# An expert block's 64 places dealt over eight groups of eight, in place of filled from the lowest

## The chip, the cores and the metric

The kernel runs on one core of one Trainium2 chip. The metric is the device time of one execution, in microseconds (us). Before the change three runs gave 1841.0, 1848.68 and 1850.56 us, median 1848.68 us.

## What is computed

Two layers of a transformer-like block in float32: 512 latent tokens and 256 context tokens of width 1024 go through convolutions, attention and a mixture of experts. Only the mixture matters here. Each token picks one of 4 groups and in it 2 of 8 experts; the tokens are sorted by expert, each expert's rows are padded to whole blocks, and each block goes through that expert's three matrices:

```python
eid = (grp[:, None] * N_PER_GROUP + top_i).reshape(-1)
order = jnp.argsort(eid)
...
buf = jnp.zeros((n_blocks * MOE_BLOCK, shp[-1]), t.dtype).at[dest].set(t[tok_sorted])
...
hdn = jax.nn.silu(xb @ e_gate[e]) * (xb @ e_up[e])
return hdn @ e_down[e]
...
y = ybuf[dest] * gate.reshape(-1)[order][:, None].astype(t.dtype)
out = jnp.zeros_like(t).at[tok_sorted].add(y)
```

The first layer has 768 tokens (1536 rows for experts), the second 512 (1024 rows). In which place of its block a row stands has no influence on the result.

## The kernel before

**Blocks.** A block has B = 64 places. An expert gets one block for each 64 rows, at least one. A row of 1024 numbers is cut into two halves of 512 (2 KB each): the half 0 of place r stands in SBUF partition r, the half 1 in partition 64 + r, so a block fills the tile `xg` of 128 partitions by 512 numbers. With the router's choices on the given inputs the blocks hold these numbers of rows, in the order in which they are worked on (an expert with more than 64 rows has several blocks):

```
first layer, 38 blocks: 47 33 41 51 41 23 41 39 61 22 64 2 38 64 40 64 30 64 64 37 36 29 26 24 38 15 32 25 21 54 45 35 64 7 59 55 50 55
second layer, 33 blocks: 21 35 55 19 46 37 12 39 46 33 3 28 64 12 54 33 21 8 28 62 48 16 42 1 43 24 14 17 22 61 41 6 33
```

**Routing** (`route`, lines 1437 to 1515, on VectorE). Every row gets a destination: its block, and its place in the block, `dest_r`, which counts 0, 1, 2 ... in the order of the rows. A one-hot table `hot_r` (line 1488) has a column for each place; it compares `dest_r` with the constant `slot`, whose column c holds c. A matmul of `hot_r` with a second table `hot_q` gives `list_gather` and `list_scatter`: for each of the 128 partitions and each block, the number of the half row that stands there. A place that no row fills gets a number out of bounds.

**Expert loop.** For each block, TensorE (`experts`, from line 916) multiplies by gate, up and down, taking turns with the transposes of the next block's `xg` (line 920). GpSimd gathers the rows of the block after that from HBM (line 1953, the list copied by line 1950) and scatters the results `y_rows` to HBM (line 1961), each with one indirect DMA of 128 partitions. Indices out of bounds move nothing:

```python
po.indirect_dma_start(out=xg, out_offset=None, in_=h2_dram[layer],
                      in_offset=bass.IndirectOffsetOnAxis(ap=idx_gather[:, 0:1], axis=0),
                      bounds_check=2 * tiles * P - 1, oob_is_err=False).then_inc(gathered[layer], 16)
```

**Weights.** SyncE loads each expert's gate, up and down (2 MB each, line 493) into nine slots, three experts' worth; the slots of expert e are loaded again for expert e + 3 as soon as the last block of expert e has been through that matrix (`reload`, line 504). TensorE waits for each piece in `weights_in`. A DMA is split over 16 DMA engines and is done when the last of them is; the indirect DMAs use the same 16 engines through a queue of their own.

Of the kernel before, what the change touches and what calls it, by code (L numbers as in the profile page):

```python
# [13 lines left out]
P = 128  # L14
# [5 lines left out]
XT, CT = S // P, C // P  # L20
NT = XT + CT
TOK = S + C
HD = 64
# [3 lines left out]
NE = NG * NPG  # L27
DE = 512
B = 64
# [8 lines left out]
CONST = {}  # L38
_at = 0
for _name, _width in (("ident", P), ("ones", P), ("before", P), ("mask_prev", P), ("mask_next", P),  # L40
                      ("cos", XT * HD), ("sin", XT * HD), ("slot", B), ("name", NE),
                      ("token", NT), ("half", 1), ("select", 2), ("eps", 1)):
    CONST[_name] = (_at, _width)
    _at += _width
# [110 lines left out]
def hybrid_flow_block(nc, x, ctx_tokens, conditions, consts, smalls, rows, w_mod, w_in, w_out, w_router,  # L155
                      e_gate, e_up, e_down, out):
    stack = ExitStack()
    with stack:
# [60 lines left out]
        hot_r = r2[:, 4608:5376].rearrange("p (a r) -> p a r", a=2 * NT)  # L219
# [63 lines left out]
        def cst(name):  # L283
            a, n = CONST[name]
            return const[:, a:a + n]
# [71 lines left out]
        def tiles_of(layer):  # L357

            return NT if layer == 0 else XT
# [675 lines left out]
        def _(ve):  # L1035
# [401 lines left out]
            def route(layer):  # L1437

                t = tiles_of(layer)
# [45 lines left out]
                nc.vector.tensor_tensor(hot, hot, value.rearrange("p c i -> p (c i)").unsqueeze(2).to_broadcast([P, 2 * t, width]),  # L1485
                                        ALU.mult).then_inc(hot_q_ready, 1)
                for c in range(2):
                    nc.vector.tensor_tensor(hot_r[:, c * t:(c + 1) * t, :], cst("slot").unsqueeze(1).to_broadcast([P, t, B]),
                                            dest_r[:, c * t:(c + 1) * t].unsqueeze(2).to_broadcast([P, t, B]),
                                            ALU.is_equal).then_inc(hot_r_ready, 1)  # L1490
                own(nc.vector.tensor_scalar(blk_table[0:1, 0:NE + 1], begins[0:1, :], 1.0 / B, None, ALU.mult))
# [88 lines left out]
            for layer in range(DEPTH):  # L1580
# [46 lines left out]
                for i in (tiles - 2, tiles - 1):  # L1627
                    choose_first(layer, i)
                    choose_second(layer, i)
                route(layer)  # L1630
                experts(layer)
                if layer == DEPTH - 1:
# [377 lines left out]
def shape_constants():  # L2010

    import numpy as np

    c = np.zeros((P, N_CONST), np.float32)

    def put(name, values):
        a, n = CONST[name]
        c[:, a:a + n] = values

    p = np.arange(P, dtype=np.float32)[:, None]  # L2020
    f = np.arange(P, dtype=np.float32)[None, :]
    put("ident", p == f)
    put("ones", 1.0)
    put("before", p < f)
    put("mask_prev", np.where(f < p, NEG, 0.0))
    put("mask_next", np.where(f > p, NEG, 0.0))
    half = HD // 2
    inv = np.float32(ROPE_THETA) ** (-np.arange(0, half, 2, dtype=np.float32) / np.float32(half))
    token = np.arange(S)
    ar = (token // GRID_W).astype(np.float32)[:, None] * inv  # L2030
    ac = (token % GRID_W).astype(np.float32)[:, None] * inv
    angle = np.concatenate([ar, ar, ac, ac], axis=-1)
    sign = np.tile(np.repeat(np.float32([-1, 1]), half // 2), 2)
    put("cos", np.cos(angle).reshape(XT, P, HD).transpose(1, 0, 2).reshape(P, -1))
    put("sin", (np.sin(angle) * sign).reshape(XT, P, HD).transpose(1, 0, 2).reshape(P, -1))
    put("slot", np.arange(B))
    put("name", np.arange(NE) - 1000)
    put("token", p + P * np.arange(NT) + 1)
    put("half", p // B)
    put("select", (p % 32) == np.arange(2))  # L2040
    put("eps", EPS)
    return c
# [66 lines left out]
```

## Time and profile before

| what | value |
|---|---|
| median of 3 runs | 1848.68 us |
| the profiled execution, its own time | 1849.2 us |
| its span, first to last instruction | 1847.6 us |
| TensorE busy | 1621.6 us (88%) |
| share of the chain that ended last: TensorE / DMA | 63% / 27% |
| expert loop of the first layer | about 520 to 1006 us |
| expert loop of the second layer | about 1357 to 1822 us |

In the profile, the chain follows the program back from its end: at each step to the work that released it. The DMA line shows the mean busy share of the 16 DMA engines in tenths, the line of GB/s below it what they moved. In a window of the DMA view, the packets of each queue are counted with their bytes and with the time they took as a share of 16 engines; q1 carries the weights, q0 the gathers and scatters.

### The profile page before, as it was taken

What the parts mean: (1) busy time and instruction counts of PE and PEld (TensorE: products, weight loads), DVE (VectorE), ACT (ScalarE), POOL (GpSimd) and SP (SyncE); (2) the same over time, 40 slices, a digit from 0 to 9 for tenths busy, and PEclk for the clock granted to TensorE, in tenths of its full rate; (3) what the DMA queues carried; (4) which work ended last, traced back from release to release, by engine and by line L of the source; (5) the groups of instructions that cost most, each with busy time, mean ns of one, the idle gap of its engine ahead of it and who ended that gap; (6) DMA issues with size and microseconds to landing.
All of it is one profiled execution on the core that took longest, in us unless ns stands there. A gap on an engine that the chain in (4) does not pass through costs nothing.

```text
span 1847.6 us, 27090 instructions
## 1 busy us (share of the span) xinstructions
PE 1621.6 (88%) x9896; PEld 942.9 (51%) x9897; DVE 647.8 (35%) x1643; ACT 310.9 (17%) x709; POOL 219.7 (12%) x346
## 2 busy tenths in 40 slices
PE   5999998999779899999796899899879979787784
PEld 3555445744456556665453444575446546344442
DVE  2094645533722222222122776552531111111113
ACT  4111115731200000000000411372300000000000
POOL 0000000000012122222111000000012112111111
PEclk9999999999879999999999899999979999999997
DMA  9358146021569999899998702302479999999995
GB/s 386 168 207 369 67 205 277 5 69 68 203 266 426 427 424 426 339 425 426 427 425 340 301 0 96 132 1 75 181 292 426 425 426 425 426 427 425 427 425 205
DMA packets 55001, 530.67 MB, mean 287 GB/s; under 512 B 12056, under 2 KB 12728, under 8 KB 25504
## 3 DMA queue, kind: packets, MB, share of 16 engines
q1 hardware_dynamic: 37760, 492.26, 63.7%
q0 software_dynamic: 14432, 27.15, 3.9%
q10 hardware_dynamic: 2752, 10.49, 1.5%
q8 instruction: 38, 0.62, 0.1%
q14 instruction: 19, 0.16, 0.0%
HBM read 520.85 MB, written 26.28 MB: 296 GB/s over the span
## 4 chain that ended last, share of the span: by engine, by line
PE 63%; DMA 27%; DVE 7%; ACT 2%; issue 1%; ACTq 0%; SPq 0%; POOLq 0%; DVEq 0%
PE ps L932 24%; DMA ring<-in_e_down_dram 13%; DMA ring<-in_e_up_dram 11%; PE ps L655 10%; PE ps L688 7%; PE ps L878 5%; PE ps L734 3%; PE ps L782 3%; PE ps L605 3%; PE ps L803 2%; DMA r<-y_dram 1%; PE ps L920 1%; PE ps L969 1%; DVE r L1531 1%; PE ps L627 1%
## 5 line engine op out<-in xcount | busy, mean ns | idle before, releaser
L932 PE MATMUL ps<-ring,r 128*64 128x256 f32 (+1 forms) x3888 | 535.7, 431 | 71.9 <-DMA ring<-in_e_up_dram 34.4
L932 PEld LDWEIGHTS ps<-ring,r 128*64 128x64 f32 x3888 | 312.1, 139 | 279.9 <-issue 132.2
L932 PE MATMUL ps<-r 128*64 128x256 f32 (+1 forms) x1768 | 241.0, 425 | 30.9 <-DMA r<-in_e_up_dram 14.8
L1528 DVE TENSOR_TENSOR r<-r,ps 128x128 f32<-128x128 f32 x142 | 34.4, 284 | 541.6 <-PE ps L932 541.6
L932 PEld LDWEIGHTS ps<-r 128*64 128x64 f32 x1768 | 142.5, 138 | 121.3 <-issue 54.5
L655 PE MATMUL ps<-r,ring 128*128 128x512 f32 (+1 forms) x480 | 177.9, 530 | 3.7 <-ACT r L1671 2.1
L688 PE MATMUL ps<-ring,r 128*128 128x512 f32 (+1 forms) x384 | 158.4, 567 | 0.0
L878 PE MATMUL ps<-ring,r 128*128 128x512 f32 x320 | 142.9, 603 | 0.8 <-DVE r L1324 0.8
L655 PEld LDWEIGHTS ps<-r,ring 128*128 128x128 f32 x480 | 91.2, 192 | 91.9 <-issue 81.2
L1548 DVE TENSOR_TENSOR r<-ps,r 128x512 f32<-128x512 f32 x71 | 49.1, 692 | 211.2 <-PE ps L932 211.2
L1838 ACT ACTIVATE r<-ps 128x256 f32<-128x256 f32 x71 | 27.2, 383 | 548.2 <-PE ps L932 548.2
L688 PEld LDWEIGHTS ps<-ring,r 128*128 128x128 f32 x384 | 72.8, 194 | 80.4 <-issue 77.5
L1196 DVE SCALAR_TENSOR_TENSOR r<-r,small 128x512 f32<-128x512 f32 (+1 forms) x180 | 104.6, 660 | 0.0
L1961 POOL DMA_INDIRECT y_dram<-r,idx_scatter x71 | 73.6, 1037 | 222.0 <-DVE r L1548 222.0
L878 PEld LDWEIGHTS ps<-ring,r 128*128 128x128 f32 x320 | 60.6, 193 | 73.9 <-issue 72.5
L1953 POOL DMA_INDIRECT r<-h_dram,idx_gather x73 | 86.1, 1180 | 63.4 <-POOL idx_gather L1950 59.6
L1294 DVE TENSOR_REDUCE stat<-ps 128x1 f32<-128x768 f32 (+3 forms) x80 | 61.3, 766 | 63.4 <-PE ps L771 40.3
L1842 ACT COPY r<-ps 128x128 f32<-128x128 f32 x71 | 18.8, 265 | 352.9 <-PE ps L969 352.9
L1950 POOL COPY idx_gather<-list_gather 128x1 uint32 (+1 forms) x73 | 13.4, 183 | 486.9 <-PE ps L920 486.9
L920 PE MATMUL ps<-const,r 128*128 128x128 f32 x292 | 60.4, 290 | 9.9 <-DMA r<-h_dram,list_gather 9.9
L782 PE MATMUL ps<-const,r 128*128 128x128 f32 x368 | 59.1, 291 | 8.9 <-ACT r L1775 4.7
L1775 ACT ACTIVATE r<-ps,stat 128x768 f32<-128x768 f32 (+3 forms) x80 | 60.5, 756 | 15.5 <-DVE stat L1300 8.2
(217 smaller groups left out, 1305.0 us busy)
## 6 DMA issues: line engine op xcount, KB each, us to landing
ring<-in_e_up_dram SPq DMA_DIRECT2D x44, 2048.0 KB, 35.1
ring<-in_e_down_dram SPq DMA_DIRECT2D x44, 2048.0 KB, 35.4
ring<-in_e_gate_dram SPq DMA_DIRECT2D x43, 2048.0 KB, 32.6
ring<-in_w_mod_dram SPq DMA_DIRECT2D x24, 2048.0 KB, 17.7
r<-in_e_gate_dram SPq DMA_DIRECT2D x20, 2048.0 KB, 35.9
r<-in_e_up_dram SPq DMA_DIRECT2D x20, 2048.0 KB, 38.2
r<-in_e_down_dram SPq DMA_DIRECT2D x20, 2048.0 KB, 38.4
ring<-in_w_in_dram SPq DMA_DIRECT2D x8, 2048.0 KB, 20.2
```

Source lines behind the costliest of these rows:

```text
L605: mm = pe.matmul(ps[32 * g:32 * g + 32, mod_bank(n), :], cond[:, 2 * g + k, :], w[:, 2 * g + k, :], start=(k == 0), stop=(k == 1), tile_po ...
L655: mm = pe.matmul(ps[:, (ct % 2) * 2 + j, 0:tn], w[:, k, col:col + P], h1T[:, t0 // P:(t0 + tn) // P, k, :], start=(k == 0), stop=(k == KD ...
L688: mm = pe.matmul(ps[:, 4 + u % 2, c0:512], h1T[:, i, k, :], chunk_ap(layer, n)[:, k, c0:512], start=(k == 0), stop=(k == KD - 1))
L782: mm = pe.transpose(ps_flat[:, 3072 + n * P:3072 + (n + 1) * P], prob[:, u % 2, n * P:(n + 1) * P], ident)
L878: mm = pe.matmul(ps[:, u % 2, :], catT[:, k, i * P:(i + 1) * P], w[:, k, :], start=(k == 0), stop=(k == 7))
L920: return pe.transpose(ps[:, 4, j * P:(j + 1) * P], xg[:, j * P:(j + 1) * P], ident)
L932: mm = pe.matmul(ps[g * B:(g + 1) * B, bank, 0:width], x, w[:, k, g * width:(g + 1) * width], start=(k == first), stop=(k == last), tile_p ...
L1196: ins = nc.vector.scalar_tensor_tensor(out=dst, in0=src, scalar=wt, in1=dst, op0=ALU.mult, op1=ALU.add)
L1294: own(nc.vector.tensor_reduce(stat[:, u % 4, 3:4], ps_flat[:, at:at + len(tiles) * P], AX.X, ALU.max))
L1775: nc.scalar.activation(prob[:, u % 2, 0:n], ps_flat[:, at:at + n], ACT.Exp, bias=stat[:, u % 4, 0:1], scale=SCALE, accum_out=stat[:, u % 4 ...
L1953: po.indirect_dma_start(out=xg, out_offset=None, in_=h2_dram[layer], in_offset=bass.IndirectOffsetOnAxis(ap=idx_gather[:, 0:1], axis=0), b ...
L1961: po.indirect_dma_start(out=y_dram[layer], in_=y_rows, in_offset=None, out_offset=bass.IndirectOffsetOnAxis(ap=idx_scatter[:, 0:1], axis=0 ...
```

## The change

A second constant, `place`, of the same width as `slot`, holds in column c the number c % 8 * 8 + c // 8. The one-hot table of the places compares with it instead of with `slot`. So the row with count v in its block now stands in place (v % 8) * 8 + v // 8: rows 0 to 7 go to the places 0, 8, 16, ... 56, rows 8 to 15 to the places 1, 9, 17, ... 57, and so on. Of n rows, the group of places 8g to 8g + 7 gets those counted g, g + 8, g + 16, ..., from its lowest place on. Gather list, scatter list, and the block in SBUF are permuted alike.

```diff
-                      ("cos", XT * HD), ("sin", XT * HD), ("slot", B), ("name", NE),
+                      ("cos", XT * HD), ("sin", XT * HD), ("slot", B), ("place", B), ("name", NE),
...
-                    nc.vector.tensor_tensor(hot_r[:, c * t:(c + 1) * t, :], cst("slot").unsqueeze(1).to_broadcast([P, t, B]),
+                    nc.vector.tensor_tensor(hot_r[:, c * t:(c + 1) * t, :], cst("place").unsqueeze(1).to_broadcast([P, t, B]),
                                             dest_r[:, c * t:(c + 1) * t].unsqueeze(2).to_broadcast([P, t, B]),
                                             ALU.is_equal).then_inc(hot_r_ready, 1)
...
     put("slot", np.arange(B))
+    put("place", np.arange(B) % 8 * 8 + np.arange(B) // 8)
```

No engine gets another instruction or another order. The one instruction of another size is the first DMA of SyncE, which brings the constants at the start of the program:

```order
 L459 UNCONDITIONAL_BRANCH
-L461 DMA const<-in_consts_dram 128x1258
+L461 DMA const<-in_consts_dram 128x1322
 L462 DMA small<-in_smalls_dram 128x2x162
 L463 DMA cond<-in_conditions_dram 128x256
```

It carries 64 more columns of 128 partitions, 32 KB.

## Rows read from the trace of the kernel before

**Rows 1.** The page, parts 1 and 2: span, and 40 equal slices of it.

```profile
span 1847.6 us, 27090 instructions
...
DMA  9358146021569999899998702302479999999995
```

**Rows 2.** Windows of the expert loops: length, busy time by engine, clock, DMA share, GB/s.

```profile
core 0: us, PE busy (x) PEld busy (x) DVE busy (x) ACT busy (x) POOL busy (x), PEclk, DMA share, GB/s
520.00:757.00 237.00, 225.00 (x1638) 139.53 (x1640) 55.32 (x135) 12.32 (x38) 52.29 (x77) 0.98 0.95 400
...
1400.00:1800.00 400.00, 336.37 (x2406) 190.42 (x2402) 57.84 (x140) 18.12 (x57) 68.48 (x112) 0.99 1.01 426
```

**Rows 3.** Chain in order of time: start, length, what.

```profile
619.48 39.73 DMA ring<-in_e_down_dram
659.25 10.56 PE ps L932 x80
...
894.77 42.08 DMA ring<-in_e_down_dram
...
964.26 36.76 DMA ring<-in_e_down_dram
1001.11 3.67 PE ps L932 x16
...
1764.99 41.76 DMA ring<-in_e_down_dram
```

**Rows 4.** DMA view, end of the second layer's loop, 1798 to 1820 us, 40 slices.

```profile
DMA  9999897898766756455544342222311100000001
GB/s 387 387 447 447 365 439 313 376 406 373 328 298 268 298 238 268 209 238 238 239 179 209 149 179 119 119 119 89 120 75 60 60 22 8 0 0 0 0 0 30
...
q1 hardware_dynamic: 299, 4.23, 45.0%
q0 software_dynamic: 267, 0.19, 2.7%
```

**Rows 5.** DMA view, end of the first layer's loop, 985 to 1008 us.

```profile
DMA  9899999999999999989997998767643321100000
...
q1 hardware_dynamic: 478, 6.82, 69.6%
q0 software_dynamic: 249, 0.21, 2.6%
```

**Rows 6.** DMA view, 740 to 780 us.

```profile
DMA  9999999999663220220033979999989999899999
```

**Rows 7.** DMA view, 1825.55 to 1825.93 us: start of the last scatter (33 rows).

```profile
DMA packets 33, 0.13 MB, mean 350 GB/s; under 512 B 0, under 2 KB 0, under 8 KB 33
...
q0 software_dynamic: 33, 0.13, 90.3%
```

**Rows 8.** DMA view, 524.40 to 524.85 us: start of a gather of 33 rows.

```profile
DMA packets 20, 0.08 MB, mean 182 GB/s; under 512 B 0, under 2 KB 0, under 8 KB 20
```

**Rows 9.** DMA view, 525.25 to 525.40 us: the same gather's last engine.

```profile
DMA packets 3, 0.00 MB, mean 14 GB/s; under 512 B 2, under 2 KB 2, under 8 KB 3
```

**Rows 10.** DMA view, 520 to 1006 us: q0.

```profile
q0 software_dynamic: 6080, 12.19, 6.5%
```

**Rows 11.** Gathers of line 1953: from issue to landing, all of 560 to 980 us.

```profile
DMA to landing us min/median/max: 3.4/8.6/9.1
```

**Rows 12.** The same, for the gather of 2 rows issued at 646.2 us.

```profile
DMA to landing us min/median/max: 8.1/8.1/8.1
```

**Rows 13.** Timeline, 695 to 706 us: issue of a gather of 64 rows, and the transposes that need it.

```profile
695.61 1.31 POOL L1953 DMA_INDIRECT r<-h_dram,idx_gather  x1 [0.84 <-POOL idx_gather L1950]
...
705.21 0.55 PE L920 MATMUL ps<-const,r 128*128 128x128 f32 x3
```

**Rows 14.** The page, part 6: the DMA of the constants.

```profile
const<-in_consts_dram SPq DMA_DIRECT2D x1, 629.0 KB, 4.0
```

## The prediction

> **What bounds the kernel now.** I read the page first: nothing but permuted data passes through the engines, so the question is where DMA decides. The DMA engines are full, at nines, over most of the two expert loops [rows 1]. The windows say how full: from 1400 to 1800 us the sixteen engines are busy all the time (share 1.01) and move 426 GB/s, while TensorE is busy 336 of 400 us at a clock of 0.99 [rows 2]. In the first loop, up to 757 us, DMA has a little air (0.95) and TensorE almost none (225 of 237 us busy) [rows 2]; about 752 to 760 us the engines run dry, because no slot is free [rows 6]. The chain agrees: its steps through weight loads of some 40 us end at 659 us, at 1001 us and at 1807 us, and TensorE goes on right behind them [rows 3]. So three times the end of a weight load sets the time: once early in the first loop, and at the end of each loop.
>
> A weight load ends when the last of its 16 parts ends, and here the view to look at is the end of each loop, where nothing more is queued. From 1798 us on the DMA share doesn't fall at once; it goes down a staircase, 9 to 0 over 15 us [rows 4]: some engines are done at 1801 us, others at 1816.4 us. Yet all had equal shares of the weights. In that window 4.23 + 0.19 MB move; at 426 GB/s all engines together need 10.4 us, so if the work lay evenly they would end at 1808.4 us. The slowest is **8.0 us** behind the mean. The first loop ends likewise: 6.82 + 0.21 MB need 16.5 us, even end 1001.5 us, real end about 1005.1 us (35 slices of 0.575 us), **3.6 us** behind [rows 5]. What differs between engines is the gathers and scatters, and the change deals exactly these anew.
>
> **Which engine carries which places.** Two windows of 33-row transfers tell. The last scatter begins with 33 packets, all of them data and none empty [rows 7]; so does a gather, 20 packets with none under 512 B [rows 8]. A packet is a pair of neighbouring places. Were eight consecutive places one engine's, the engines of places 40 to 63 (six of the sixteen) would have empty pairs alone and begin with these. They begin with data, all sixteen. The last engine of that gather ends on one half-full packet, one empty and its completion [rows 9]: the pair of places 32, 33, then the empty pair 34, 35, and nothing more. So an engine's places end with 32 to 35 as a run of four, behind data. I take it that each engine has two runs of four, at the same place in each 32: 0 to 3 with 32 to 35, 4 to 7 with 36 to 39, and so on, eight engines for each half row.
>
> The size of the staircase tests this. A full pair took 0.903 × 16 × 0.38 us / 33 = 0.166 us [rows 7], a row's half 0.083 us. In the second loop, over the gathers of blocks 3 to 33 and the scatters of blocks 1 to 31, the engine with places 0 to 3 and 32 to 35 carries 352 rows, the mean engine 244: 108 × 0.083 = 9.0 us, measured 8.0. With eight consecutive places, the first engine would carry 470 rows and be 18.8 us behind. In the first loop, counted from where the engines ran dry, 214 against 161 rows: 4.4 us, measured 3.6. Runs of four it is.
>
> The rows leave the pairing of the runs open. The Trainium skill, page "DMA: Bandwidth & Descriptors", section "The descriptor swizzle", states it for a plain transfer over 128 partitions: partitions 0 to 3 with 32 to 35 on engine 0, the next four with 36 to 39 on engine 1, partitions 64 and up on engines 8 to 15. No run here shows it for indirect transfers beyond the runs of four; it is the pairing I took, and it speaks against this change: with it the sum is the one below, with a pairing shifted by one run the second rival's.
>
> **The change part by part.** *The dealing.* Of n rows each group of eight places now fills from its lowest place. Its first four places lie with one engine, its last four with the next; both runs of an engine are then either first fours or last fours. Up to n = 32, eight of the sixteen engines carry everything and eight nothing. The heaviest carried min(4, n) + min(4, n − 32 if positive); it now carries min(4, n/8 rounded up) + min(4, (n − 4)/8 rounded up). For 36 rows and more both give 8; for 25 to 32 it is 7 or 8 in place of 4; at 16 it is 4 and 4, below that less than before (12 rows: 3 in place of 4). Summed over the list of blocks, the heaviest goes from 250 to 277 rows in the first layer and from 186 to 204 in the second. It is the heaviest engine that decides, not the mean: while it has a queue, its own work sets the end.
>
> Only what lies ahead of a deciding wait counts. Up to 659 us (gathers 3 to 12, scatters 1 to 10): 3 + 7 = 10 more rows. From the dry spell to 1001 us (gathers 22 to 38, scatters 20 to 37): 17 + 17 = 34. Second loop, as above: 15 + 17 = 32. Together 76 × 0.083 = **6.3 us**. The early 0.8 us of it isn't lost again in the dry spell, as TensorE is the bound there and shifts whole.
>
> Bounds: a row at the weights' own rate, 2048 B / (426/16 GB/s), costs 0.077 us; by the whole first loop's gathers and scatters, 0.065 × 16 × 486 us for 12.19 MB [rows 10], 0.085 us. The staircases came to 0.82 and 0.89 of what the count gives, which makes 5.2 us the lower end; all 45 rows both ways at 0.085 us, 7.7 us, is the upper.
>
> *Transfers with nothing beside them.* The second layer's first gather (21 rows) has three data packets on its heaviest engine for two, its last scatter (33 rows) four for two: 3 × 0.166 = 0.5 us, both waited for. *Half-full pairs* become more frequent; a half packet costs its half, nothing. *Constants*: 32 KB more on 629 KB in 4.0 us [rows 14], at most 0.2 us, taken as 0.1 us, ahead of the first tokens. *VectorE's compare*: same size and count, nothing. *Other gathers* in the loops: hidden, see the last rival.
>
> Sum 6.3 + 0.5 + 0.1 = 6.9 us by the count; scaled down a little toward the staircases, **+6.5 us**. Against the profiled execution's own 1849.2 us that is 1855.7 us; the median of the runs is 0.5 us lower, so 1855 us.
>
> **Rivals.** *1. The heaviest engine isn't what decides* (later loads give the lag back, or TensorE has slack I didn't see): no change, about 1849 us. For it: TensorE is the bound over half of the loops. Against: the chain's three long loads [rows 3]. *2. Even load after all:* if runs are paired shifted, so that first and last fours share an engine, every engine gets the mean. Then the lags go: 8.0 us, 3.6 us, and before 659 us some 2.6 us (37 rows over the mean × 0.083 × 0.85): up to 14 us, less a small rest, about 1836 us. Against: nothing in rows 7 to 9 suggests a shift. *3. Slower, by the gather's own latency.* The next block's transposes need a gather 9.6 us after its issue (695.61 to 705.21 us) [rows 13]; the longest gathers land in 9.1 us [rows 11]. Now eight engines, not one or two, carry four data packets, each taking turns with weights. If the latest lands 0.5 us beyond that limit in each of some 40 blocks that TensorE bounds, 20 us are lost: 1869 us; below 9.6 us it costs nothing. Against: a gather of 2 rows lands in 8.1 us [rows 12], all with 64 rows, four packets everywhere, within the 9.1 us, and no block after the change carries more.
>
> **How the numbers follow.** A measurement of this kernel can tell about 0.5%, 9.2 us, from no change. Forecast 0.68, rival 1 0.15, rival 2 0.11, rival 3 0.06. Forecast and rival 1 both lie within 0.5%, but for a rest from the runs' spread (1841.0 to 1850.56 us): faster 0.13, same 0.77, slower 0.10. The forecast's bounds with its small terms, +5 to +8 us, make 1854 to 1857 us; with that spread and rival 1 the range is 1846 to 1862 us, leaving out rivals 2 and 3.
>
> **What would show it.** Right: a last scatter of 33 rows that begins with empty packets and has engines with four data packets; a longer staircase at both ends (lags near 10.7 and 6.4 us); TensorE's waits for weights up by some 6 us; gathers within 9.2 us. Wrong: a staircase that is gone and a time near 1836 us (rival 2); transposes waiting for gathers (rival 3); a longer staircase at an unchanged time (rival 1).

## The result, and the profile after

Nine runs of the changed kernel have a median of 1857.63 us, nine of the kernel before 1848.68 us; the ratio is 1.0054 with a 95% interval of 1.0038 to 1.0070. The change makes the kernel slower by 9 us, 0.5%, and the whole interval lies above 1; forecast were 6.5 us. A second measurement (below) gave 1.0047, 1.0031 to 1.0062.

The page after, span and DMA share; the DMA line answers to that of [rows 1]:

```profile
span 1856.0 us, 27090 instructions
...
DMA  9459146011669999799997702302479999999995
```

The chain says where the 8.4 us of span are. From the kernel before, the four steps that bound the two expert loops (start, length, what), then the chain of the kernel after with the steps that answer to [rows 3]:

```profile
517.00 3.32 DMA r<-h_dram,list_gather
...
1006.43 2.72 DMA y_dram<-r,idx_scatter
...
1353.23 2.87 DMA r<-h_dram,list_gather
...
1823.98 2.46 DMA y_dram<-r,idx_scatter
```

```profile
515.04 3.36 DMA r<-h_dram,list_gather
...
617.53 42.02 DMA ring<-in_e_down_dram
659.60 10.56 PE ps L932 x80
...
962.21 37.12 DMA ring<-in_e_up_dram
999.37 5.25 PE ps L932 x32
1005.90 3.67 PE ps L932 x16
1011.22 2.73 DMA y_dram<-r,idx_scatter
...
1358.28 3.03 DMA r<-h_dram,list_gather
...
1773.16 41.71 DMA ring<-in_e_down_dram
...
1832.09 2.73 DMA y_dram<-r,idx_scatter
```

From the first gather to the last scatter the first loop took 1006.43 − 517.00 = 489.4 us, now 496.2 us (+6.8); the second 470.8, now 473.8 us (+3.1). What lies ahead of the first loop became 2 us shorter, which is chance (below). Within the first loop, 142.25 us passed up to the matmuls behind the early wait (659.25 − 517.00), now 144.56 us (+2.3), and from there to the last down matmuls 341.9, now 346.3 us (+4.4).

The staircase at the end of the second loop (DMA view, 1800 to 1830 us, slices of 0.75 us; it answers to [rows 4]) shows the mechanism at a glance:

```profile
DMA  9998755575445455554555545454542000000000
...
q1 hardware_dynamic: 372, 5.29, 41.3%
q0 software_dynamic: 400, 0.33, 3.2%
```

It is no staircase any more, but one step: from 1803 to 1824 us the share stays at about a half. By the prediction's count for this loop, eight engines carried 368 to 384 rows, the other eight 100 to 128. The 5.62 MB need 13.2 us at 426 GB/s, an even end would be 1813.2 us; the heavy half is **10.8 us** behind it, where 10.7 were forecast. The same at the end of the first loop (985 to 1008 us before [rows 5], 985 to 1012 us here, slices of 0.675 us), 7.14 MB, even end 1001.8 us, real end about 1009.0 us (the last packet of 16 KB starts at 1008.4 us and takes 0.6 us), 7.2 us behind, 6.4 forecast. Read to the end of its last packet, the first loop before ended at 1005.4 us, 3.9 us behind, where the prediction has 3.6:

```profile
DMA  9999999999999997754455564445555451000000
...
q1 hardware_dynamic: 475, 6.73, 58.6%
q0 software_dynamic: 315, 0.41, 4.2%
```

And the last scatter, again 33 rows, begins with empty packets now, 12 of its first 20, where 33 of 33 held data [rows 7] (DMA view, 1833.70 to 1833.80 us):

```profile
DMA packets 20, 0.03 MB, mean 288 GB/s; under 512 B 12, under 2 KB 12, under 8 KB 20
```

### The profile page after: what moved, and what is told of

Read it like the earlier page. It is cut to its first block, busy times and chain, and to the rows that moved or that the text cites. A ratio compares the mean times of both kernels' runs of the same rounds, so it can differ in the third digit from the quotient of the medians.

```text
span 1856.0 us, 27090 instructions
## 1 busy us (share of the span) xinstructions
PE 1623.1 (87%) x9896; PEld 940.1 (51%) x9897; DVE 647.8 (35%) x1643; ACT 311.4 (17%) x709; POOL 219.9 (12%) x346
## 4 chain that ended last, share of the span: by engine, by line
PE 62%; DMA 27%; DVE 7%; ACT 2%; issue 1%; ACTq 0%; SPq 0%; POOLq 0%; DVEq 0%
PE ps L932 24%; DMA ring<-in_e_down_dram 13%; DMA ring<-in_e_up_dram 11%; PE ps L655 9%; PE ps L688 7%; PE ps L878 5%; PE ps L734 3%; PE ps L782 3%; PE ps L605 2%; PE ps L803 2%; DMA r<-y_dram 1%; PE ps L920 1%; PE ps L969 1%; DVE r L1531 1%; PE ps L627 1%
```

## The experiments

All eight were timed in five rounds against the kernel before. The table has the ratios and, from the chain of each profile, the length of the loops (last scatter's issue less first gather's) and of the stretch up to the matmuls behind the early wait. "Rows" is the count of the prediction for the heaviest engine, first loop (both stretches) and second.

| kernel | rows | ratio (95%) | first loop | of it up to the early wait | second loop |
|---|---|---|---|---|---|
| before | 349 + 352 | 1 | 489.4 | 142.3 | 470.8 |
| constant only | 349 + 352 | 1.0004 (0.9989 to 1.0018) | 490.0 | 142.9 | 470.8 |
| the change | 393 + 384 | 1.0054 (1.0038 to 1.0070) | 496.2 | 144.6 | 473.8 |
| the change again | 393 + 384 | 1.0047 (1.0031 to 1.0062) | 495.0 | 144.3 | 474.3 |
| first loop only | 393 + 352 | 1.0027 (1.0015 to 1.0039) | 496.0 | 144.3 | 470.7 |
| second loop only | 349 + 384 | 1.0021 (1.0008 to 1.0033) | 489.4 | 142.1 | 473.9 |
| from the top | 393 + 384 | 1.0046 (1.0030 to 1.0063) | 493.9 | 144.2 | 474.0 |
| one engine after another | 432 + 470 | 1.0089 (1.0068 to 1.0111) | 495.7 | 143.9 | 478.8 |
| even by runs | 281 + 270 | 0.9956 (0.9939 to 0.9973) | 485.7 | 141.0 | 465.1 |
| even there and back | 262 + 250 | 0.9944 (0.9925 to 0.9963) | 486.3 | 141.2 | 465.6 |

**Even by runs.** The rows are dealt to the eight sets of places that the prediction ascribes to one engine each.

```diff
-    put("place", np.arange(B) % 8 * 8 + np.arange(B) // 8)
+    run = np.arange(B) // 4 % 8
+    turn = np.arange(B) % 4 + 4 * (np.arange(B) // 32)
+    put("place", turn * 8 + run)
```

> The change's table replaced by one that deals the rows in turn to eight sets of eight places, a set being two runs of four: 0 to 3 with 32 to 35, 4 to 7 with 36 to 39, and so on. Theory A (the engine with the most rows ends each weight load last; an engine carries two runs of four at the same place in each 32): in the three stretches counted the heaviest engine carries 108 + 173 + 270 = 551 rows in place of 701 before and 777 with the change, so 150 x 0.083 = 12.5 us less than before, 18.8 us less than the change; the staircase at the end of the second loop shrinks to a lag of some 2 us. Theory B (what the change costs is the gathers' own landing, for which TensorE waits): the kernel before has no such wait, so this one is no faster than before; near 1849 us. Theory C (any dealing that isn't consecutive costs): slower than before, like the change.

1838.67 against 1847.25 us: faster than before, so theories B and C fall. The end of its second loop (1785 to 1815 us, slices of 0.75 us):

```profile
DMA  9999999999999989999998856200000000000004
...
q1 hardware_dynamic: 512, 7.34, 57.6%
q0 software_dynamic: 471, 0.43, 4.2%
```

The engines end together, 7.77 MB would do so at 1803.2 us, the last at about 1805.2 us: 2.0 us behind. That bears out that an engine's places are a run of four in the first 32 and one in the last 32 (with eight consecutive places an engine, this dealing would leave 12.6 us by the count). It doesn't say which two runs share an engine: with the pairing shifted by any number of runs, the heaviest engine has 258 to 270 rows in the second loop. "One engine after another" below tells the pairings apart. The gain, 8.6 us by the medians, is less than the 12.5 us of the count.

**Constant only.**

```diff
-    put("place", np.arange(B) % 8 * 8 + np.arange(B) // 8)
+    put("place", np.arange(B))
```

> The extra constant is kept, but holds 0 to 63, so the rows stand as before. Theories A and B: as before within 0.2%, at most 0.2 us for the 32 KB. Theory D (part of the 9 us comes from the longer constants or from what they shift): slower by a few us.

No difference, and loops as before to 0.6 us. Theory D falls: it is the dealing.

**One engine after another.**

```diff
-    put("place", np.arange(B) % 8 * 8 + np.arange(B) // 8)
+    run = np.arange(B) // 4 % 8
+    turn = np.arange(B) % 4 + 4 * (np.arange(B) // 32)
+    put("place", run * 8 + turn)
```

> The opposite dealing: the first eight rows all go to the places 0 to 3 and 32 to 35, the next eight to 4 to 7 and 36 to 39, and so on. Theory A: heaviest engine 154 + 278 + 470 = 902 rows against 701 before: 201 x 0.083 = 16.7 us slower than before, about 1865 us, and a staircase at the end of the second loop of some 19 us of lag. Theory B: the fullest engine has four data packets per gather from eight rows on, as in a full block: no more than the change, 0 to 9 us. Theory C: about the same as the change.

16.4 us slower by the ratio, 16.7 expected, 14.3 us by the medians. Its staircase (1785 to 1830 us, slices of 1.125 us) is the longest of all:

```profile
DMA  9999799797676665565544434222221110000000
...
q1 hardware_dynamic: 608, 8.75, 46.4%
q0 software_dynamic: 560, 0.60, 3.7%
```

9.35 MB, even end 1806.9 us, last weights about 1823.3 us: 16.4 us behind. Put side by side for the second loop: the lags are 2.0, 8.0, 10.8 and 16.4 us (even, before, change, one after another), that is −6.0, 0, +2.8 and +8.4 us; the loops' lengths differ by −5.6, 0, +3.1 and +8.0 us. The loop's time follows the last engine's lag one for one, to within 0.4 us.

These lags also tell which pairing it is, which the rows before had left open. Had the runs of the last 32 places been shifted by an odd number against those of the first, the change would have dealt evenly, to about 1 us, and left no plateau. With a shift by two, four or six runs, the heaviest engine would carry 342 to 410 rows in this run's second loop and be 8.1 to 13.8 us behind by the count; with no shift it carries 470 and is 18.7 us behind. Measured were 16.4 us, 0.88 of the last, as the 8.0 us before are 0.89 of their 9.0. The Trainium skill's rule for a plain transfer ("DMA: Bandwidth & Descriptors", section "The descriptor swizzle") thus holds here for gathers and scatters through the index list, as to which partitions share an engine; the engines' numbers the traces don't show.

**Even there and back.**

```diff
-    put("place", turn * 8 + run)
+    put("place", turn * 8 + np.where(turn % 2 == 0, run, 7 - run))
```

(The first line is that of the even dealing by runs.)

> As the even dealing by runs, but every second round of eight goes through the sets backwards, so that the rows left over don't always fall to the same first sets. Theory A: heaviest engine 99 + 163 + 250 = 512 rows (the mean is 503): 39 x 0.083 = 3.2 us less than the even dealing, 15.7 us less than before, about 1833 us. If the last lags don't matter (another limit takes over), the same time as the even dealing.

0.9944 beside 0.9956, with loops no shorter: no gain over the plain even dealing, although the rows are level to 250 against a mean of 244. The end of its second loop (1785 to 1815 us) looks the same, too: 7.69 MB, even end 1803.1 us, last weights about 1805.3 us, 2.2 us behind where the count leaves 0.5 us.

```profile
DMA  9999998999999999999999953100000000000003
...
q1 hardware_dynamic: 507, 7.26, 57.1%
q0 software_dynamic: 425, 0.43, 4.3%
```

Something else sets the last 2 us. What it is wasn't tried; a candidate stands below. This is the fastest of the kernels here by its ratio, 1838.62 us, and the two even ones can't be told apart.

**First loop only, second loop only, and the change again.** The first two choose the constant by layer:

```diff
-cst("place").unsqueeze(1)
+cst("slot" if layer else "place").unsqueeze(1)
```

and the other way round.

> The change's dealing in the first layer alone; the second layer keeps the rows from the lowest place. Theory A by count: 44 more rows on the heaviest engine x 0.083 = 3.7 us in the first loop, none in the second (470.8 us from its first gather to its last scatter, as before). Theory E (in the first loop there is more than the count: about 1.5 us up to the wait near 660 us, because other small loads meet a heavy engine, and 1.6 us at its end, because TensorE waits before its up matmuls and runs them at a lower clock): the first loop again some 6 to 7 us longer than before, 495 to 497 us in place of 489.4 us.

> The change's dealing in the second layer alone. Theory A: first loop as before (489 to 490 us), second loop 32 more rows x 0.083 = 2.7 us longer (473.5 us), in all 2.7 to 3.5 us or 0.15 to 0.2% slower than before. Theory E: the same here. Theory B (gathers' landing): the same amount in both loops by blocks, so about half of the change's 9 to 10 us.

> The change itself once more, for a second profile. Theory A by count: first loop 493 us, second 473.5 us. Theory E: first loop 495 to 497 us with the up matmuls at its end at a lower clock again. If the first loop comes out near 493 us, its surplus in the first profile was that execution's.

Each loop lengthens only where the dealing is changed: the second by 3.1 to 3.6 us in all of them, near the 2.7 us of the count; the first by 5.6 to 6.8 us, where the count says 3.7 us. Theory E holds as to the amount, and that the first loop loses twice what the second does, with 38 blocks against 33, speaks against theory B once more. As to the reasons of E, one is seen. In the first profile of the change and in that of "first loop only" TensorE waits at the loop's end for the last expert's up matrix (2.21 and 2.24 us before the first of its matmuls); the next 32 up matmuls then take 5.25 and 5.36 us where they took 3.67 us at this place before. (Before, too, 32 up matmuls behind a wait of 2 us are as slow, 5.36 us at 884.46 us for one; but there TensorE has further loads to wait for, while at the loop's end the time is not made up.) From the timeline after, gate and up of that expert:

```profile
993.49 3.67 PE L932 MATMUL ps<-ring,r 128*64 128x256 f32 x32 [1.11 <-DMA ring<-in_e_gate_dram]
999.37 5.25 PE L932 MATMUL ps<-ring,r 128*64 128x256 f32 x32 [2.21 <-DMA ring<-in_e_up_dram]
```

The windows of that stretch, after and then before (length, busy times, granted clock, DMA share, GB/s), show TensorE's granted clock: in the five microseconds of which it was busy for 2.79 us it is 0.92 on average, in the next five 0.74, so the matmuls from 999.37 us on ran at 1.2 GHz for a part of the time and at 2.4 GHz for the rest; before, where the same matmuls ran from 995.59 to 999.26 us, it stayed at 1.00, 2.4 GHz:

```profile
995.00:1000.00 5.00, 2.79 (x25) 1.82 (x22) 0.00 (x0) 0.38 (x1) 0.21 (x1) 0.92 0.57 237
1000.00:1005.00 5.00, 5.00 (x35) 2.78 (x31) 0.25 (x2) 0.00 (x0) 0.00 (x0) 0.74 0.52 220
```

```profile
995.00:1000.00 5.00, 4.42 (x38) 2.81 (x38) 0.48 (x2) 0.00 (x0) 0.00 (x0) 1.00 0.92 388
1000.00:1005.00 5.00, 3.92 (x19) 1.32 (x17) 1.83 (x5) 0.27 (x1) 1.68 (x3) 1.00 0.41 174
```

The chain runs through these matmuls, so up to 1.6 us of the first loop's surplus in these two profiles can be theirs; no run here took the slow clock away alone. In "the change again" the longest wait at that place came one matrix earlier, the same up matmuls took 3.67 us, and the loop was 1.2 us shorter.

**From the top.** The groups fill from their highest place, so the other eight engines are the heavy ones.

```diff
-    put("place", np.arange(B) % 8 * 8 + np.arange(B) // 8)
+    put("place", (7 - np.arange(B) % 8) * 8 + np.arange(B) // 8)
```

> The change's dealing mirrored: each group of eight places is filled from its highest place down, so that the other eight engines (places 4 to 7 with 36 to 39 and so on) are the heavy ones, with the same numbers of rows. Theory A: the same time as the change, +0.3 to +0.6%. Theory E's part on other small loads: if these sit on engines that the change makes heavy, here they meet light ones, and the stretch up to the wait near 660 us is some 1.5 us shorter than with the change (143 in place of 144.6 us from the loop's first gather); if it is as long, the small loads aren't the reason.

The same time as the change, as theory A has it, but the stretch up to the early wait is as long, 144.2 us. So E's other reason, small loads on just the engines that the change makes heavy, isn't borne out. The four profiles with the change in the first loop have 144.2 to 144.6 us there, the three without it 142.1 to 142.9 us: 1.3 to 2.5 us more, where the count says 0.8 us. In the first profile all of it lies in the down load that the wait is for (39.73 us before, 42.02 us after); what lies between the loop's first gather and the issue of that load takes 102.5 us in both. Why the load takes more than the count says stays open.

## Why the prediction was right

**What bounds the loops** was right in the main: waits for weight loads, whose end moves with the rows of the heaviest engine. They are more than the three named, though. The chain before goes through four weight loads in the first loop and seven in the second (the load from 894.77 us, in [rows 3], is one of those between). If the heaviest engine's queue carries its lag from one load to the next, as the one-for-one of lag and loop length suggests, the count up to the last wait stands. Right too was the reading of a fours-and-fours layout from three narrow windows, against the eights that the change's table suggests: the kernel slows down, the packets of the last scatter and both lags came out near the forecast (10.8 and 7.2 us for 10.7 and 6.4), and the half-full plateau is the two classes of engines that the step "eight of the sixteen engines carry everything" describes. Two small slips leave the sums as they are: with 13 to 15 rows the heaviest engine carries four, as before, not less; and the three data packets of the gather of 21 rows are two full and two half-full ones.

The prediction took the end of the staircase for the deciding wait, "where nothing more is queued". It isn't. In the second loop before, TensorE's last wait, for the last but one expert's down matrix, is over at 1806.85 us, ten microseconds ahead of the staircase's end at 1816.4 us; the last expert's up and down matrices, which end there, are not waited for (timeline of TensorE before, 1740 to 1826 us):

```profile
1806.85 3.65 PE L932 MATMUL ps<-ring,r 128*64 128x512 f32 x16 [0.65 <-DMA ring<-in_e_down_dram]
...
1813.76 3.65 PE L932 MATMUL ps<-ring,r 128*64 128x256 f32 x32
...
1818.66 3.65 PE L932 MATMUL ps<-ring,r 128*64 128x512 f32 x16 [0.26 <-DVE r L1531]
```

In the first loop, what ends at 1005 us is a load of `w_in` for the next layer (issued at 979.53 us); the wait for the last down matrix was over at 1001.1 us [rows 3]. So a lag read from the staircase is that of the slowest engine's queue at its end, not of the load that is waited for. That it still gives the loop's change is what the four lags beside the four loop lengths show.

**The term that was mis-sized** is the first loop's: 3.6 us in the step "only what lies ahead of a deciding wait counts" (0.8 up to 659 us, 2.8 from the dry spell on). Measured were 5.6 to 6.8 us in three profiles, 4.5 us with the mirrored dealing. At its end the count of the lag was right and what came behind the wait was missing: in two profiles of four the chain's last wait moved from the down to the up matrix, and TensorE took 1.6 us longer for the 32 matmuls behind it. The second loop's 2.7 us came out at 3.1 to 3.6 us. The small term of the transfers with nothing beside them held: the second layer's first gather went from 2.87 to 3.03 us and its last scatter from 2.46 to 2.73 us, together 0.4 us for 0.5. The sum, forecast at 6.5 us, was some 9 us, inside the range. That range, 1846 to 1862 us, also holds the unchanged time, so lying in it says little; the lags and packets bear out the mechanism.

**The sign of TensorE's waits** ("up by some 6 us") held in sum and not in its parts. Its waits for weights rose from 26.1 to 32.3 us in the first loop, but went from 62.8 to 61.7 us in the second. There TensorE was busy 3.4 us longer for the same matmuls, at a lower mean clock. The clock isn't needed as a second cause: with the change in the second loop only, the loop is as long (473.9 us), while TensorE is busy hardly longer than before and waits 2.6 us more. The loads set the loop's length; it differs whether TensorE spends the time waiting or at the lower clock (windows from the second loop's first gather to its last scatter: before, after, and with the change there only):

```profile
1353.23:1823.98 470.75, 398.35 (x2842) 228.46 (x2842) 68.86 (x167) 22.25 (x67) 82.01 (x135) 0.98 0.95 401
```

```profile
1358.28:1832.09 473.81, 401.71 (x2842) 228.99 (x2842) 68.88 (x167) 22.30 (x67) 82.04 (x134) 0.97 0.95 398
```

```profile
1352.68:1826.58 473.90, 398.67 (x2842) 227.38 (x2842) 68.83 (x167) 22.31 (x67) 82.21 (x135) 0.98 0.94 398
```

**Rival 1** (the heaviest engine doesn't decide) fell with the one-for-one of lag and loop length. **Rival 2** (even load) fell with the plateau, and the two even dealings show what it would have been: 8 to 10 us gained, not 14. The count overstates what levelling gives: 12.5 us in the plain one and 15.7 us there and back, where a rest of some 2 us stays that the count doesn't have. **Rival 3** (the gather's latency) was true in miniature. The longest gathers grew from 9.2 us to 9.8 us in the first profile of the change, and to 10.3 us in the second, where TensorE once waited for one (all gathers of line 1953 from 525 to 1800 us: before, after, and in "the change again"; then the timeline of the last):

```profile
DMA to landing us min/median/max: 3.0/8.4/9.2
```

```profile
DMA to landing us min/median/max: 2.8/8.4/9.8
```

```profile
DMA to landing us min/median/max: 3.3/8.3/10.3
```

```profile
546.67 1.29 POOL L1953 DMA_INDIRECT r<-h_dram,idx_gather  x1 [0.84 <-POOL idx_gather L1950]
...
557.05 0.55 PE L920 MATMUL ps<-const,r 128*128 128x128 f32 x3 [0.73 <-DMA r<-h_dram,idx_gather]
```

The sign "gathers within 9.2 us" was therefore wrong, but the price is 0.73 us once (with the mirrored dealing 0.39 and 0.46 us), not 20 us: the median gather, 8.4 us, stays below the limit of 9.6 us.

## What to carry to other kernels

Where weight loads fill the DMA engines, look at how their share falls at the end of a stage: a staircase or a plateau says that some engines carry more than others, and the end against total bytes by full rate says how many microseconds levelling could give at most: of the 8.0 us at the end of the second loop here, the even dealing took back 5.6. Before dealing work over DMA engines, find out which partitions share one, by a transfer that fills a known part of them; here it is runs of four, 32 apart, and a table made for runs of eight made it worse. And count the heaviest engine, not the mean: the mean is 244 rows in the second loop for every dealing here, and the loop's length ranges from 465.1 to 478.8 us.

## What had not been expected

The time ahead of the first loop's first gather, in which the kernels do the same work, was anything from 508.6 us (constant only) to 517.8 us (the change again) in the ten profiles, while the second loop of equal dealings agrees to 0.1 us without the change (470.8, 470.8, 470.7) and to 0.5 us with it (473.8, 473.9, 474.3). So most of the spread between profiles lies ahead of the loops, and the chain's stretches tell changes of a microsecond or two apart that the total can't.

Loads of instructions are small, but each is one packet on a single engine. One of them in the first loop of the changed kernel (DMA view, 536.7 to 538.0 us) moved 16 KB:

```profile
q8 instruction: 1, 0.02, 4.8%
```

0.048 × 16 × 1.3 us = 1.0 us of one engine, as much as 12 rows. Three or four such fall into the second layer's loop; they may be the rest of 2 us that even dealing leaves, which no run here tested.
